# Two layers with a mixture of experts on one core: tokens of the second pair by indirect load, experts by counting, other slots and another last order

## What is computed

```
g_prob = softmax(xt @ w_group + b_group);  g_w, g_idx = top_k(g_prob, 1)            # 4 groups
e_sel  = the chosen group's 4 of (xt @ w_expert + b_expert)                          # 16 experts
e_w, e_idx = top_k(softmax(e_sel), 2);  e_w = e_w / sum(e_w)
y = sum over the two chosen experts of  g_w * e_w * ((silu(xt @ w_gate) * (xt @ w_up)) @ w_down)
```

## Time and profile before

| | |
|---|---|
| time, median of 3 runs (lowest, highest) | 1206.75 us (1202.06, 1208.33) |
| the profiled execution's own time, its span | 1206.32 us, 1204.5 us |
| busy: TensorE, DVE, ACT, POOL | 94%, 35%, 19%, 10% |
| DMA moved | 317.08 MB, mean 263 GB/s |
| experts of layer 0, from the first gather to the last product | 423 to 665 us |
| experts of layer 1, the same | 950 to 1194 us |

### The profile page before, as it was taken

How to read it: one execution, slowest core, us unless ns; L and a number is a source line. 1 busy time by engine, 2 the same in 40 slices (tenths; PEclk the granted TensorE clock), 3 DMA queues, 4 the chain that set the end, 5 groups by cost and what they waited for, 6 DMA issues and landing times.

```text
span 1204.5 us, 20026 instructions
## 1 busy us (share of the span) xinstructions
PE 1126.8 (94%) x8604; PEld 674.0 (56%) x8604; DVE 416.9 (35%) x1086; ACT 228.6 (19%) x530; POOL 118.4 (10%) x213
## 2 busy tenths in 40 slices
PE   4999999997999899999998999989989999999985
PEld 1666666664444676666663444435545766665642
DVE  2165556555613330000103654217733510001105
ACT  3211110110221411111111311127712311111110
POOL 0343344333000000000001000000000000000001
PEclk9999999999999999999999999999989999999998
DMA  9985354436931369999998942237741399999994
GB/s 347 305 268 162 94 148 134 141 141 232 409 115 50 140 251 375 425 424 426 427 425 318 388 156 70 97 147 266 255 179 70 104 374 426 425 424 427 425 389 150
DMA packets 100737, 317.08 MB, mean 263 GB/s; under 512 B 3856, under 2 KB 38976, under 8 KB 85280
## 3 DMA queue, kind: packets, MB, share of 16 engines
q1 hardware_dynamic: 93296, 298.05, 64.7%
q10 hardware_dynamic: 5248, 10.97, 2.3%
q0 software_dynamic: 2096, 6.67, 1.7%
HBM read 304.67 MB, written 11.01 MB: 262 GB/s over the span
## 4 chain that ended last, share of the span: by engine, by line
PE 77%; DMA 14%; DVE 4%; ACT 2%; issue 2%; SPq 0%; POOL 0%; ACTq 0%; DVEq 0%
PE bank L695 13%; PE bank L844 11%; PE bank L1041 10%; PE bank L719 7%; PE bank L605 7%; PE bank L684 5%; PE bank L500 4%; PE bank L853 4%; PE bank L971 3%; DMA ring<-in_moe_w_up 3%; DMA moe_ring<-in_moe_w_up 3%; DMA ring<-in_moe_w_down 3%; DMA moe_ring<-in_moe_w_down 3%; DMA ring<-in_w_ada 2%; PE bank L869 2%
## 5 line engine op out<-in xcount | busy, mean ns | idle before, releaser
L695 PE MATMUL bank<-ring,xn 128*64 128x256 f32 x1536 | 170.3, 380 | 3.9 <-DMA ring<-in_moe_w_up 3.0
L695 PEld LDWEIGHTS bank<-ring,xn 128*64 128x64 f32 x1536 | 110.7, 137 | 66.3 <-issue 7.9
L844 PE MATMUL bank<-uT,ring 128*128 128x384 f32 x384 | 135.1, 496 | 0.0
L1041 PE MATMUL bank<-ring,uT 128*128 128x512 f32 x288 | 126.9, 594 | 2.9 <-ACT uT L1150 1.6
L1750 DVE TENSOR_TENSOR moe_hh<-xn,bank 128x256 f32<-128x256 f32 x32 | 13.5, 421 | 298.2 <-ACT xn L1234 298.2
L844 PEld LDWEIGHTS bank<-uT,ring 128*128 128x128 f32 x384 | 69.2, 190 | 42.4 <-issue 2.2
L684 PE MATMUL bank<-moe_g,moe_h 128*128 128x128 f32 x768 | 92.2, 277 | 0.4 <-DVE moe_g L1644 0.4
L684 PEld LDWEIGHTS bank<-moe_g,moe_h 128*128 128x128 f32 x768 | 88.2, 192 | 6.1 <-issue 6.1
L1041 PEld LDWEIGHTS bank<-ring,uT 128*128 128x128 f32 x288 | 53.4, 190 | 66.3 <-issue 65.2
L719 PE MATMUL bank<-ring,xn 128*64 128x512 f32 x384 | 86.0, 599 | 1.9 <-DMA ring<-in_moe_w_down 1.9
L2138 POOL TENSOR_TENSOR moe_flag<-con 128x1 f32<-128x1 f32 x2 | 0.4, 193 | 856.8 <-DMA ring<-in_moe_w_down 856.8
(11 more groups left out here) (274 smaller groups left out, 1267.8 us busy)
## 6 DMA issues: line engine op xcount, KB each, us to landing
ring<-in_w_ada SPq DMA_DIRECT2D x24, 2048.0 KB, 10.7
ring<-in_moe_w_gate SPq DMA_DIRECT2D x24, 2048.0 KB, 18.1
ring<-in_moe_w_up SPq DMA_DIRECT2D x24, 2048.0 KB, 22.3
ring<-in_moe_w_down SPq DMA_DIRECT2D x20, 2048.0 KB, 25.5
ring<-in_hgrn_w_in SPq DMA_DIRECT2D x32, 512.0 KB, 7.7
moe_ring<-in_moe_w_gate SPq DMA_DIRECT2D x8, 2048.0 KB, 22.5
moe_ring<-in_moe_w_up SPq DMA_DIRECT2D x8, 2048.0 KB, 24.2
moe_ring<-in_moe_w_down SPq DMA_DIRECT2D x8, 2048.0 KB, 20.8
```

Source lines behind the costliest of these rows:

```text
L695: last = mm(bank[2 + e][64 * g:64 * g + 64, 256 * part:256 * part + 256], m["xe"][:, k, 64 * e:64 * e + 64], cols(slot)[:, k, 256 * g:256 ...
L844: last = mm(to[:, 0:TOK], w[:, k, f, :], uT[:, k, :], start=(k == 0), stop=(k == KC - 1))
L1041: last = mm(bank[b % 2][:, :], uT[:, k, t * P:(t + 1) * P], cols(slot)[:, k, :], start=(k == 0), stop=(k == KC - 1))
```

## The change

Four edits are joined.

1. *The second pair's tokens by indirect load.* POOL stores `h` to a table in HBM, tile by tile, as ACT has copied it. TensorE multiplies the second pair's one-hots (made into `gw`) with the numbers of the tokens, between the two halves of the first gather; DVE casts the sum to integers; POOL fetches the 128 rows from the table into tile 1 of `own`. The second pair's gather is then eight transposes of these rows.
2. *Experts by counting.* For each group of four logits the position in the order is counted: how many are above, and how many are equal and stand ahead. Position 0 of the groups and positions 0 and 1 of the experts give the selection. Centred logits for the softmax and the two one-hots by rank come later, behind the first pairs' one-hots and in `places`. Fillers go from 10 to 2 and from 4 to 3.
3. *Other slots for the early modulation blocks:* 4, 0, 5, 4 in place of 4, 5, 4, 5; blocks 2 and 3 are multiplied one part earlier; the wait of L977 goes, and the output weights' second block waits for slot 5's fifth release in place of the sixth.
4. *The end of the stage.* Tile 1's fetched rows of the first half take the place of the two fillers, those of the second half stand ahead of the last pair's; every half has its own count; DVE takes the halves in another order, and layer 1 stores tiles 0, 2, 1.

```diff
-LAST_MM = 2 + T
+LAST_MM = 4 + T
 WRITES = PAIRS - 1
+FETCHED = 1
+GATHERS = 2 * PAIRS + FETCHED
+ONEHOTS = PAIRS + FETCHED
+ROWS_IN = (32, 48, 32)
...
-    put("first", np.tile([4, 3, 2, 1], (P, 1)))
+    put("lower", np.tile((np.arange(4)[None, :] < np.arange(4)[:, None]).reshape(1, 16), (P, 1)))
...
+    put("token", np.arange(T)[None, :] * P + i[:, None])
...
+        EARLY_SLOTS = ((4, 4, 240), (0, 5, 96), (5, 4, 272), (4, 5, 256))
...
-                ada(1, 4 + b % 2, b, 4 + b // 2)
+                slot, before, _ = EARLY_SLOTS[b]
+                ada(1, slot, b, before)
             for b in range(2):
-                block512(0, 4 + b, a["hgrn_w_out"][0], b, 6)
+                block512(0, 4 + b, a["hgrn_w_out"][0], b, 6 - b)
...
+            for at_tile, t in enumerate((0, 2, 1)):
+                sp.wait_ge(S[1]["added"], count * T + at_tile)
...
+                elif part == 3:
+                    early_product(2)
                 elif part == 4:
-                    early_product(2)
+                    early_turn(2)
                 elif part == 5:
-                    early_turn(2)
+                    early_product(3)
                 elif part == 6:
-                    early_product(3)
-                elif part == 7:
                     early_turn(3)
...
-                keep_busy(10, P)
+                keep_busy(2, P)
...
-                keep_busy(4, P)
+                keep_busy(3, P)
...
+                def tokens_of(i):
+
+                    pe.wait_ge(s["onehot"], onehots_made(at_pass[0], i))
+                    for t in range(T):
+                        last = mm(bank[4][:, 0:1], m["gw"][:, t, :, :], const("token")[:, t:t + 1],
+                                  start=(t == 0), stop=(t == T - 1))
+                    last.then_inc(s["gathered"], 1)
+
+                def gather(half, i):
 
                     if half == 0:
-                        pe.wait_ge(s["onehot"], it + 1)
+                        if 1 <= i <= FETCHED:
+                            pe.wait_ge(s[f"rows{i}"], at_pass[0] * ROWS_IN[i] + 16)
+                        else:
+                            pe.wait_ge(s["onehot"], onehots_made(at_pass[0], i))
                     for k in range(4):
+                        if 1 <= i <= FETCHED:
+                            here = slice((4 * half + k) * P, (4 * half + k + 1) * P)
+                            last = nc.tensor.transpose(bank[half][:, k * P:(k + 1) * P], m["own"][:, i, here], ident)
+                            continue
...
-                            keep_busy(2, 512, 7)
+                            fetched_rows(0, False, True).then_inc(s["last_mm"], 1)
...
                     last_pair(0, 0, True, True).then_inc(s["last_mm"], 1)
+                    last_pair(2, 0, True, True).then_inc(s["last_mm"], 1)
                     last_pair(1, 0, True, False)
-                    last_pair(2, 0, True, True)
-
-                def fetched_rows(half):
+
+                def fetched_rows(half, start, stop):
 
                     here = slice(512 * half, 512 * half + 512)
+                    if half == 0:
+                        pe.wait_ge(s["rows1"], at_pass[0] * ROWS_IN[1] + ROWS_IN[1])
                     for j, rows in enumerate((m["own"], second_rows[n])):
                         done = mm(bank[LAST_BANKS[1][half]][:, :], m["rw"][:, j, :], rows[:, 1, here],
-                                  start=False, stop=(j == 1))
+                                  start=(start and j == 0), stop=(stop and j == 1))
...
-                    base = p * PAIRS
-                    gather(0, base)
-                    gather(1, base)
+                    gather(0, 0)
+                    tokens_of(1)
+                    gather(1, 0)
 
                 def after(p):
 
                     pe.wait_ge(s["oe_ready"], p * (2 * PAIRS) + 2 * PAIRS)
                     last_pair(0, 1, True, True).then_inc(s["last_mm"], 1)
                     last_pair(2, 1, True, True).then_inc(s["last_mm"], 1)
-                    last_pair(1, 1, True, False)
-                    pe.wait_ge(s["rows1"], p * 32 + 32)
-                    fetched_rows(0)
-                    fetched_rows(1).then_inc(s["last_mm"], 1)
+                    fetched_rows(1, True, False)
+                    last_pair(1, 1, False, True).then_inc(s["last_mm"], 1)
...
-            need(pe, 1, "mod_cols", EARLY)
...
+                fives = m["lg"][:, :, :].rearrange("p t (r j) -> p (t r) j", j=4)
+                each = fives.unsqueeze(3).broadcast_to([P, 5 * T, 4, 4])
+                against = fives.unsqueeze(2).broadcast_to([P, 5 * T, 4, 4])
+                lower = const("lower").rearrange("p (j i) -> p j i", j=4).unsqueeze(1).broadcast_to([P, 5 * T, 4, 4])
+                v.tensor_tensor(m["equal"][:, :, :, :], against, each, ALU.is_equal)
+                own(v.tensor_tensor(m["above"][:, :, :, :], against, each, ALU.is_gt))
+                own(v.tensor_tensor(m["equal"][:, :, :, :], m["equal"][:, :, :, :], lower, ALU.mult))
+                own(v.tensor_tensor(m["above"][:, :, :, :], m["above"][:, :, :, :], m["equal"][:, :, :, :], ALU.add))
+                own(v.tensor_reduce(m["order"][:, :, :], m["above"][:, :, :, :], X_AXIS, ALU.add))
+                order = m["order"][:, :, :].rearrange("p (t r) j -> p t r j", r=5)
+                in_group = t4[:, 2, :, :].unsqueeze(3).broadcast_to([P, T, 4, 4])
+                own(v.tensor_scalar(t4[:, 2, :, :], order[:, :, 0, :], 0.0, None, ALU.is_equal))
+                v.scalar_tensor_tensor(m["sel"][:, 0:T, :].rearrange("p t (g j) -> p t g j", g=4), order[:, :, 1:5, :], 2.0,
+                                       in_group, ALU.is_lt, ALU.mult).then_inc(s["selected"], 1)
+
+                def logits_centred():
+
+                    gl = m["lg"][:, :, 0:4]
+                    el = m["lg"][:, :, 4:20].rearrange("p t (g j) -> p t g j", g=4)
+                    own(v.tensor_reduce(t1[:, 0, :], gl, X_AXIS, ALU.max))
+                    v.tensor_tensor(t4[:, 0, :, :], gl, b4(t1[:, 0, :]), ALU.subtract).then_inc(s["group_centred"], 1)
+                    own(v.tensor_tensor(t16[:, :, :, :], el, in_group, ALU.mult))
+                    own(v.tensor_reduce(t4[:, 4, :, :], t16[:, :, :, :].rearrange("p t g j -> p t j g"), X_AXIS, ALU.add))
+                    es = t4[:, 4, :, :]
+                    own(v.tensor_reduce(t1[:, 2, :], es, X_AXIS, ALU.max))
+                    v.tensor_tensor(t4[:, 5, :, :], es, b4(t1[:, 2, :]), ALU.subtract).then_inc(s["expert_centred"], 1)
+
+                def choices():
+
+                    for j, onehot in ((0, 7), (1, 9)):
+                        chosen = m["sel2"][:, j, :, :].rearrange("p t (g j) -> p t g j", g=4)
+                        own(v.scalar_tensor_tensor(chosen, order[:, :, 1:5, :], float(j), in_group, ALU.is_equal, ALU.mult))
+                        own(v.tensor_reduce(t4[:, onehot, :, :], chosen.rearrange("p t g j -> p t j g"), X_AXIS, ALU.add))
+                    own(v.tensor_tensor(t4[:, 11, :, :], t4[:, 9, :, :], t4[:, 7, :, :], ALU.add))
...
+                def tokens_of(i):
+
+                    dve.wait_ge(s["gathered"], tokens_summed(at_pass[0], i))
+                    v.tensor_copy(m["idx"][:, i - 1:i], bank[4][:, 0:1]).then_inc(s["onehot"], 1)
...
-                    onehots(0)
+                    onehots(0, m["g"])
+                    onehots(1, m["gw"])
                     if isinstance(p, int):
+                        logits_centred()
                         count_passes()
-                    rows(p * PAIRS)
+                    tokens_of(1)
+                    rows(0)
...
                     last_added(0, 0)
-                    last_added(0, 1)
                     rows_summed(2)
+                    last_added(1, 0)
                     if n == 0:
+                        last_added(0, 1)
                         next_norm(0, p)
-                    for t in range(1, T):
-                        last_added(t, 0)
-                        last_added(t, 1)
+                        last_added(1, 1)
+                        last_added(2, 0)
+                        last_added(2, 1)
+                    else:
+                        last_added(2, 0)
+                        last_added(0, 1)
+                        last_added(2, 1)
+                        last_added(1, 1)
...
+                def store_tokens():
+
+                    for t in range(T):
+                        need(pool, n, "h_act", 2 * t + 2)
+                        g.dma_start(token_table[n][t * P:(t + 1) * P, :], m["h"][:, t, :]).then_inc(s["h_stored"], 16)
+                    need(pool, n, "h_stored", 48)
+
+                def fetch(p):
+
+                    for i in range(1, FETCHED + 1):
+                        pool.wait_ge(s["onehot"], token_known(p, i))
+                        g.tensor_tensor(m["flag"][:, 1:2], ones[:, 0:1], ones[:, 0:1], ALU.mult)
+                        pool.drain()
```

(5 more changed lines are left out.)

104 lines of the change are left out of this document (41 added, 63 removed).

## The result

| | before | changed |
|---|---|---|
| median of the first comparison, us (runs) | 1204.88 (4) | 1191.51 (4) |
| its range | 1202.06 to 1208.33 | 1190.32 to 1193.28 |
| profiled execution, its span | 1206.32, 1204.5 | 1190.32, 1188.5 |

The ratio is 0.9887 [0.9865, 0.9909]; a second comparison gave 1190.73 and 0.9880 [0.9853, 0.9908]. The forecast was 1186.1, a ratio of 0.983. The direction held, and so did the range for 8 in 10 (1179 to 1194), but both medians miss the forecast's own range of 1181 to 1190, and the gain is some 13.4 us and not 20.2.

What follows compares the result with a forecast made beforehand. TensorE bounds nearly everywhere, but expert stages end when their last weights land. Terms -4.4 - 1.6 - 2 x 2.3 + 2 x 0.7 - 2 x 3.0 + 0.6 + 0 - 5.6 = -20.2 turn 1206.3 into 1186.1 us; own range 1181 to 1190.

Steps and rivals of the forecast that it cites:

- The scan: Layer 0's last scan: early modulation blocks stop waiting for slots and loads, 4.4 us gained, bounds 2.0 and 5.8.
- The output gate: Wait for four turned blocks ahead of the output gate's first product goes: 1.6 us gained, bounds 0.8 and 1.7.
- Counting and token sum: Choice of experts, each layer: counting on DVE gains 2.3 us, the added token products on TensorE lose 0.7.
- The closed hole: Expert stages: earlier weight loads end the DMA stream's standstill, 3.0 us gained per layer, bounds 0 and 3.5.
- the rival of a late fetch: Second pair's fetched rows land late behind weights, TensorE waits, kernel slower at 1212 us; chance 5%.
- The clock: Rival: half clock over a gather in both layers and after layer 0's new wait, 1190.6 us; chance 15%.
- a sign of being wrong: Stated signs: TensorE waits on fetched tokens, half-clock stretches at the gathers, or a lower stream rate in the saturated part.
- The +0.6 us: Loss charged for fewer filler products possibly letting TensorE's clock be granted at half: 0.6 us in all, bounds 0 and 3.4.
- Layer 0's end: End of layer 0's expert stage: new wait for fetched rows offset by fewer products behind, zero; bounds -1.0 and +2.5.
- Layer 1's end: End of layer 1: DVE takes tile 1's first half earlier, ends 6.1 us sooner, 0.5 given back; 5.6 us gained.
- The late modulation loads: Rival: all three early modulation weight loads overlap and stay late, the scan keeps its pace, 1190.5 us; chance 10%.

Runs made afterwards that it cites:

- slots_back: The changed kernel with early modulation blocks in their old slots and parts, the wait ahead of the output gate still gone: 1194.87 us, ratio 0.9918.
- count_undone: The changed kernel with the choice of experts done by the old chain of comparisons, with its 10 and 4 fillers: 1192.37 us, ratio 0.9899.
- fetch_undone: The changed kernel without token table, fetch and token sum, the second pair gathered by products as before: 1196.31 us, ratio 0.9939.
- after_again: The changed kernel itself once more, unchanged, as base beside other follow-up kernels on the same chip: 1190.73 us, ratio 0.9880.
- end_undone: The changed kernel with the old order at the expert stage's end in both layers: 1193.86 us, ratio 0.9898.
- branch_ahead: The changed kernel with TensorE's branch over further passes put ahead of the last pair's work, which stands in both arms: 1186.01 us, ratio 0.9845.
- the fuller heads: branch_ahead with more filler products in the waits of each layer's choice of experts: 1187.38 us, on another chip 1182.52 us.
- early_branch: The changed kernel with TensorE's branch over further passes moved ahead of the first pass's last wait and last products: 1189.22 us, ratio 0.9868.

## Why the prediction was right and wrong

*The scan: mis-sized.* "I take 4.4 us; bounds 2.0 ... and 5.8": the trace gives 2.0, the two traces of before less the mean of eleven with the new slots (20.2 us) give 2.1, and only against slots_back is it 4 and more. The waits went as forecast. What the step left out is that the half-clock block is no part of the wait for weights: it came back in seven of the eleven scans, 1.4 us each, and the four without it take 19.2 to 19.4 us; and the stop of 0.6 to 1.6 us for "issue", behind a fetch of instructions, which ten of the eleven have and before has at 0.25 us at most.

*The output gate: right in kind, small in size*: 1.6 forecast with an upper bound of 1.7, 1.89 in the trace.

*Counting and token sum: right in the traces.* 2.3 forecast, 2.35 on DVE; 0.7 forecast, 0.73 measured, with the gather 0.25 shorter. In the traces the heads gain 2.55 and 1.8 us, in the means 1.7 each, for 1.6 forecast. The times of count_undone show 1.6 us for both layers together and leave the rest open.

*The closed hole: right in kind, on the low side.* 3.0 net per layer and 3.5 at most, 3.7 and 3.6 in the traces; fetch_undone takes 4.8 to 5.6 away for both layers. The fetched rows cost no wait. Their path was mis-timed to the safe side: it took the 10.2 and 5.6 us of transfers inside the full stream, had the stores done by 424 to 429 and the rows landed by 433 to 441, where the trace has 417.25 and 427.14, ahead of the first weights. So the 0.5 us charged to the stream weren't lost, and the rival of a late fetch had no ground; how such a load fares inside the full stream, these fetches don't test.

*The clock: not against before, but a sign of being wrong came true.* "If half-clock stretches appear at the gathers": they do in after_again, in both layers, and in eight of sixteen heads of the form, though not in the first trace. They don't set the change back against before, whose four heads all have a stretch at half clock: the mean head is 1.35 us above the shortest seen in the form of the changed kernel (17.29, 15.94), and 1.25 above it in before (18.99, 17.74). The +0.6 us are neither shown nor refused. At layer 0's end the rival had named the new wait for the fetched rows; there the first trace waits 0.94 us at full clock, and the granted clock came down behind the stop at the branch, in both traces of the changed kernel.

*Layer 0's end: wrong.* "Layer 0: zero; bounds -1.0 and +2.5". The queue ended and the norm was ready as worked out; the failed step is the one after it, that TensorE starts when the norm is ready. It starts some 7.5 us after its last wait ahead of the branch, and the two products taken away (1.7 us) and the span itself, 0.6 longer, turned 0.93 us of idle time, which stood in the trace of before as "issue" at L591, into 3.25. With the half clock behind it that is 3.7 us in the traces, 2.5 by end_undone, 4.7 by branch_ahead (which also takes away what showed there before). A small slip beside it: by the step's own numbers the queue ends at 664.55 + 1.6 - 1.72 = 664.4, not 664.2.

*Layer 1's end: right*, 5.6 forecast, 5.65 in the trace. The two parts came out otherwise: 6.1 forecast on DVE and 0.5 given back for the outputs, 5.65 on DVE and 0.16 more behind it (1188.5 - 1184.35 = 4.15 in place of 3.99). Behind the last products nothing more is asked of TensorE.

Together: 6.8 us of the forecast gain are missing. Layer 0's end accounts for 3.7 of them, the scan for 2.4 and the later start for 1.4; the gate, the hole, the heads and the clock gave 3.5 more than forecast, and the remaining 2.8 lie between the two traces and their medians. The measured time is also near that of two rivals. The late modulation loads (1190.5) did not happen: no scan with the new slots waits over 0.5 us for a load. The clock (1190.6) did in part: the second trace of the changed kernel has half clock over the gather in both layers and at layer 0's end, if behind another wait than the rival named, the first trace only at layer 0's end, and the two executions took 1190.84 and 1190.32 us. A time alone doesn't tell the causes apart here. That the stop at the branch ends with the arrival of instructions is shown by the packets and by its moving with the branch; what sets the start of the fetch isn't settled.

The best version that is measured twice with one answer is branch_ahead, 1186.0 and 1186.5 us. That it meets the forecast's time is chance: it takes one more change. With the fuller heads it is perhaps 1 to 2 us less.

## What to carry to other kernels

Look for "issue" gaps at a branch in the profile before and count the work queued behind the last wait ahead of it: whoever shortens that queue uncovers the branch. The packets of kind "instruction" tell whether such a gap is a fetch. Put a branch where the engine has a long queue or waits for memory anyway, even if code must stand in both arms, and look at the clock there too. The half clock in the scan did not stay with the block that showed it, so don't book its return as part of a wait that you remove.

## What was not expected of the hardware

A branch in TensorE's program in layer 0 cost 7.1 to 8.2 us from the last wait ahead of it to the first product behind it, about the same with 4.6, 5.6 or 6.3 us of products between; in layer 1 of early_branch it was 6.35 us at most. The first product came 1.5 to 1.8 us behind the end of a 16 KB transfer of instructions, which itself took 0.9 to 1.1 us.

Stops of 2.5 to 3.5 us at the branch were followed by a granted half clock over part of the next 10 us in twelve of fourteen cases, and idle times of 0.9 to 1.4 us there in none of four. In the heads half clock came in thirteen of sixteen, with waits of 0.4 to 1.6 us, and in none of four once these were filled to 0.2 to 0.4 us. TensorE also stopped for 0.2 to 3.1 us for "issue" inside batches of 24 small records without any branch, and each of these stops ended 1.2 to 1.5 us behind a transfer of instructions.
